# Normed tiles 1280 bytes apart, with weight blocks placed modulo 512 bytes

## The chip, the cores and the metric

One core of one Trainium2 chip runs the whole kernel. The metric is the device time in microseconds (us). It is given as a median of several runs. Differences are a few parts in a thousand, so the number of runs and their spread stand beside each time.

## The reference, cut to what matters

The program is two transformer blocks on one sequence of 256 positions, with 1024 channels, all in float32. The first block has an mLSTM and latent-attention mixer, a cross attention to 256 memory rows and a feed-forward of width 4096. The second block puts 16 meta tokens ahead of the sequence, so that it works on 272 positions, until these are dropped:

```
h = concatenate([meta, x])                                   # 16 + 256 positions
h = h + 0.5 * swiglu(rmsnorm(h, ffn1_norm), w_gate, w_up, w_down)      # width 2816
u = rmsnorm(h, mix_norm)
aq, ak, av, gq, gk, gv, gr, g_low, gate_a, gate_b = split(u @ w_in)    # 4368 columns
mixed = sigmoid(gate_a) * (window_attention(...) @ w_branch_att)
      + sigmoid(gate_b) * (gated_linear_attention(...) @ w_branch_gla)
h = h + mixed @ w_out
h = h + 0.5 * swiglu(rmsnorm(h, ffn2_norm), ...)
return rmsnorm(h, final_norm)[:, 16:]
```

Nearly all the work is the matrix products with weights. Their biggest one on 272 positions is the first SwiGLU of the second block: 1024 x 5632 weights for gate and up, then 2816 x 1024 for down.

## The kernel before, in words

Activations are kept transposed: 128 channels on the partitions, positions along them. An array of 1024 channels is eight tiles `k`. A product streams the tile of activations through TensorE against a stationary block of 128 x 128 weights. For float32 accuracy each value is split into a high part (float32r, rounded) and a low part, and three matmuls add up to one product: high weights on high activations (L1055), high weights on low activations (L1056), low weights on high activations (L1057). So each product of a weight block and a tile is three matmuls in a row, of 256 or 272 streamed columns.

`U` and `UL` hold the high and low parts of the normed input (eight tiles), `H` and `HLO` those of a hidden layer (22 tiles), `Y` and `YL` those of the mixers' outputs. Where a stage works on 256 positions, tile `k` of `U` begins 1024 `k` bytes after the first (`part`, L901). Where it works on 272 (`sw1`, `in2`, `gvr`, `gab`, read by `streamed`, L907), tile `k` begins 1088 `k` bytes after it. The products that need no meta columns (`NO_META`: gq, aq, gr, ga, gb) begin 64 bytes further in and stream 256 columns.

Weights come from HBM in units of at most 1024 columns (512 KB). `Gemm.units` (L173) says which rows of tiles `k` a unit holds: with 512 columns in a group, two. SyncE issues the loads in the order of `plan.loads` into six slots `raw` (`unit`, L2444); a load waits until the split of the unit six before it is done. ScalarE writes the high parts into `wh` (L1393), VectorE the low parts into `wl` (L1819); there are four halves for units that are split and not yet used up. TensorE then goes through the tiles of a unit: four blocks of 128 columns, for each its two `k`, for each three matmuls, 24 in all (`tile`, L1029). All groups of a product run after one another.

Where the blocks of a unit lie in `wh` and `wl` is decided by `first_columns` (L256), in steps of 16 columns, 64 bytes. For the products on 272 positions it shifts the block for tile `k` until its place is the place of tile `k` in `U` modulo 256 bytes. `same_place` (L196) orders the tiles so that a unit holds `k` and `k` + 4, which lie at the same place modulo 256 bytes. The first group of `sw1`, `in2` and `gvr` (`plain=1`) keeps the order 0, 1, 2, ..., because its tiles are only just being made. For `small`, `uv`, `o`, the feed-forward of the first block, `out2`, `sw2`, `dn2` and all others, `U`, `H` and the blocks lie at one place modulo 512 bytes without a shift, and `Y` at one of two places 256 bytes apart.

The order of the work is fixed by `Plan`: `first_block` and `second_mixer` weave the products with attention, mLSTM and gated linear attention by strings of letters (L117, L125), one letter for one step; the feed-forwards run straight through, except that one matmul against a block of ones in `cst` (`rstd_sum`, L1071, L1085) stands after 12 weight tiles of `ff1a` and after 9 of `sw1` and `sw2`. The mean square of the normed input comes from it. The gate matmul of the linear attention (`gla_logits`, L1240, L1244) waits for its weights `glagw`, which SyncE loads once (L2481).

The memory of a partition is laid out in `build` by the order of the calls of `sb`; each tensor begins at a multiple of 32 bytes. `beyond` puts a filler ahead of a tensor to bring the next address to a residue; `cst` is first, 5656 bytes long from byte 1152, then `vec` and seven small tensors, then X, U, UL, Y and the rest.

Of the kernel before, what the change touches and what calls it, by code (L numbers as in the profile page):

```python
# [14 lines left out]
P = 128  # L15
D = 1024
EPS = 1e-6
T1 = 256
T2 = 272
NMETA = 16  # L20
FF1 = 4096
# [158 lines left out]
def columns(w, n, width=512, r0=0):  # L180
    per = width // P
    return [([(w, r0, width * g, width)], [(128 * j, 128, per * g + j) for j in range(per)])
            for g in range(n // width)]
# [11 lines left out]

def same_place(n):  # L196

    pairs = [(8 * i + j, 8 * i + j + 4) for i in range((n + 7) // 8) for j in range(4) if 8 * i + j + 4 < n]
    order = [k for pair in pairs for k in pair]
    return order + [k for k in range(n) if k not in order]  # L200
# [21 lines left out]
    "ff2b": Gemm(2048, columns("w_ff2", D, r0=2048)),  # L222
    "sw1": Gemm(D, swiglu_columns("ffn1_w_gate_2", "ffn1_w_up_2"), same_place(8), plain=1),
    "dn1": Gemm(FF2, columns("ffn1_w_down_2", D), same_place(22)),
    "in2": Gemm(D, [([("w_in_2", 0, 2304, 16), ("w_in_2", 0, 2304, 16), ("w_in_2", 0, 768, 256)],
# [3 lines left out]
                    ([("w_in_2", 0, 0, 512)], [(128 * j, 128, ("aq", j)) for j in range(4)])], same_place(8), plain=1),  # L229
    "gvr": Gemm(D, wide("w_in_2", (("gv", 0, 1280), ("gr", 0, 1792))), same_place(8), plain=1),  # L230
    "gab": Gemm(D, wide("w_in_2", (("ga", 0, 2320), ("ga", 4, 2832), ("gb", 0, 3344), ("gb", 4, 3856))), same_place(8)),
    "branch": Gemm(512, [([(n, 0, 512 * g, 512)], [(128 * j, 128, (kind, 4 * g + j)) for j in range(4)])
# [23 lines left out]
def first_columns(name, g, i):  # L256


    ks, width = GEMM[name].units(g)[i], GEMM[name].width(g)
    skew = {"sw1": 0, "dn1": 0, "in2": g == 2, "gvr": g, "gab": 1}.get(name)  # L260
    at, shift = [], 0
    for n, k in enumerate(ks):
        while skew is not None and (n * width // 16 + shift - k - skew) % 4:
            shift += 1
        at.append(n * width + 16 * shift)
    return at
# [634 lines left out]
def part(t, name, k, n):  # L901

    at = SL * (k // 4) + n * (k % 4) if name in ("Y", "YL") else n * k
    return t[name].rearrange("p k c -> p (k c)")[:, at:at + n]


def streamed(t, name, k, tag):  # L907

    if name in ("small", "uv", "o", "wq_x", "ff1a", "ff1b", "sw2"):
        return part(t, "U", k, T1), part(t, "UL", k, T1)  # L910
    if name in ("sw1", "in2", "gvr", "gab"):
        a = NMETA if name != "sw1" and tag[0] in NO_META else 0
        return t["U"][:, k, a:T2], t["UL"][:, k, a:T2]
    if name in ("memk", "memv", "ff2a", "ff2b", "out2", "dn2"):
        return part(t, "H", k, T1), part(t, "HLO", k, T1)
    if name == "dn1":
        return t["H"][:, k, :], t["HLO"][:, k, :]
    if name in ("uq", "ukv"):
        k = 2 if name == "ukv" else k
        return t["CQH"][:, k, :], t["CQL"][:, k, :]  # L920
    return part(t, "Y", k, T1), part(t, "YL", k, T1)
# [1518 lines left out]
def sp_program(e, t, plan, ev):  # L2440
# [31 lines left out]
    for v in range(6, len(plan.loads)):  # L2472
        unit(v)
        if plan.loads[v] == ("ff1b", 0, 0):
            e.wait_ge(*at("mlstm_log", (3, 1)))
            e.wait_ge(*at("scores_masked", 3))
            e.wait_ge(*at("mlstm_sums", 3))
            e.dma_start(cst[:, OVER:OVER + NLATE], t["d_cst"][:, NCST:NCST + NLATE]).then_inc(
                *up("in_late", 0, by=16))
            e.wait_ge(*at("mlstm_qk", 3))  # L2480
            e.dma_start(t["glagw"][:, :], t["d_glagw"]).then_inc(*up("in_gg", 0, by=16))  # L2481
# [14 lines left out]
def build(nc, aps, out):  # L2496
    with ExitStack() as ctx:
# [9 lines left out]
        t["cst"] = sb("cst", [P, NCST])  # L2507
        t["vec"] = sb("vec", [P, NVEC])
        t["gcol"] = sb("gcol", [P, 8])
        t["DC"] = sb("DC", [P, 8])  # L2510
        t["ST"] = sb("ST", [P, 2, 6])
        t["ST2"] = sb("ST2", [P, 2, 16])
        t["nsink"] = sb("nsink", [P, 8])
        t["QRS"] = sb("QRS", [P, 8])
        t["QKG"] = sb("QKG", [P, 8])
        beyond(64, 256, "before_x")
        t["X"] = sb("X", [P, 8, T2])
        base = nc.sbuf_base
        for n in ("U", "UL"):
            t[n] = sb(n, [P, 8, T2], F32R)  # L2520

# [12 lines left out]
        t["G"] = sb("G", [P, 2, T2])  # L2534
        t["RM"] = sb("RM", [P, T2])
        beyond((base + 512) % 1024, 1024, "before_h")
# [18 lines left out]
        over(top_hlo, ("GT", [P, 6, 256], F32), ("PR", [P, 2, 512], F32), ("PT", [P, 2, 512], F32))  # L2555
        over(top_hlo, ("GQ1", [P, 2 * T1], F32))
        t["glagw"] = nc.alloc_sbuf_tensor_at("glagw", [P, 256], F32, offset=nc.sbuf_base)
        t["wqk"] = sb("wqk", [P, 4, 128])
        at = nc.sbuf_base
# [96 lines left out]
```

## Time and profile before

| | |
|---|---|
| runs | 922.36, 922.81, 924.12 us (median 922.81 of 3) |
| the profiled execution's own time | 922.65 us |
| its span, first to last instruction | 920.8 us |
| mean granted TensorE clock | 0.998 |
| matmul / weight load busy | 903.7 us (98%) / 886.0 us (96%), 7443 of each |
| VectorE / ScalarE busy | 642.5 us (70%) / 527.8 us (57%) |
| HBM read | 155.11 MB, 170 GB/s over the span |

The span leaves out what lies before the first and after the last instruction, here 1.85 us. A matmul of the trace is shown longer than the distance to the next one, since matmuls overlap in the array; so the pace is read from the starts, and the shown duration only tells one kind of matmul from another.

### The profile page before, as it was taken

The page shows a single profiled execution, that of the slowest core. Times are in us where ns is not written, and L with a number is a line of the kernel's source. Part 1 is how long each engine was busy: PE and PEld are TensorE (multiplying, and loading weights), DVE is VectorE, ACT ScalarE, POOL GpSimd, SP SyncE. Part 2 cuts the span into 40 slices and gives each one's busy share as a digit, 9 for nine tenths or more (in the row PEclk, how much of TensorE's full clock was granted, in tenths as well). Part 3 has the DMA queues.
Part 4 walks back from the last instruction along what each step waited for, and adds up shares of the span by engine and source line. Part 5 has one row for each costly group of instructions (what it writes and reads, how often), then busy time and mean ns, then how long its engine had stood idle before and what let it go on. Part 6 is the DMA issues. An engine that isn't in the chain of part 4 may idle for free.

```text
span 920.8 us, 18474 instructions
## 1 busy us (share of the span) xinstructions
PE 903.7 (98%) x7443; PEld 886.0 (96%) x7443; DVE 642.5 (70%) x1092; ACT 527.8 (57%) x862; POOL 3.5 (0%) x9
## 2 busy tenths in 40 slices
PE   8999999999999999999999999999999999999996
PEld 7987999899999999999999999999999999999996
DVE  5999778777556766666666548768769867767553
ACT  5788867776436655544444435454675665454452
POOL 1000000000000000000000000000000000000000
PEclk9999999999999999999999999999999999999999
DMA  9651435265665566555556565554416665666641
GB/s 330 222 177 38 130 114 192 53 227 198 206 209 168 190 201 192 174 172 175 181 184 198 153 183 163 158 174 126 159 47 192 198 183 184 191 200 201 210 138 47
DMA packets 110292, 157.37 MB, mean 171 GB/s; under 512 B 9728, under 2 KB 61056, under 8 KB 110080
## 3 DMA queue, kind: packets, MB, share of 16 engines
q1 hardware_dynamic: 109632, 155.22, 53.5%
q8 instruction: 60, 0.98, 0.4%
q10 hardware_dynamic: 576, 0.96, 0.3%
q14 instruction: 24, 0.20, 0.1%
HBM read 155.11 MB, written 1.05 MB: 170 GB/s over the span
## 4 chain that ended last, share of the span: by engine, by line
PE 95%; DVE 2%; ACT 1%; issue 1%; DMA 1%; SPq 0%; DVEq 0%; ACTq 0%
PE ps L1055 29%; PE ps L1057 29%; PE ps L1056 29%; PE ps L1102 1%; PE ps L1138 1%; DMA X<-d_x 1%; PE ps L1314 0%; PE ps L1334 0%; DVE wl L1819 0%; PE ps L1272 0%; PE ps L1335 0%; ACT wh L1393 0%; PE ps L1294 0%; PE ps L1148 0%; PE ps L1161 0%
## 5 line engine op out<-in xcount | busy, mean ns | idle before, releaser
L1819 DVE TENSOR_TENSOR wl<-raw,wh 128x1024 fp32r<-128x1024 f32 (+2 forms) x291 | 346.1, 1212 | 192.3 <-ACT wh L1393 192.0
L1393 ACT ACTIVATE wh<-raw 128x1024 fp32r<-128x1024 f32 (+2 forms) x291 | 297.9, 1046 | 190.7 <-PE ps L1057 190.3
L1055 PE MATMUL ps<-U,wh 128*128 128x256 f32 (+2 forms) x1392 | 396.5, 285 | 4.9 <-DVE wl L1819 3.3
L1057 PE MATMUL ps<-U,wl 128*128 128x256 f32 (+2 forms) x1392 | 390.3, 280 | 0.0
L1056 PE MATMUL ps<-UL,wh 128*128 128x256 f32 (+2 forms) x1392 | 389.6, 280 | 0.0
L1055 PEld LDWEIGHTS ps<-U,wh 128*128 128x128 f32 (+1 forms) x1392 | 261.7, 188 | 8.0 <-DVE wl L1819 6.3
L1056 PEld LDWEIGHTS ps<-UL,wh 128*128 128x128 f32 (+1 forms) x1392 | 261.7, 188 | 1.1 <-issue 0.5
L1057 PEld LDWEIGHTS ps<-U,wl 128*128 128x128 f32 (+1 forms) x1392 | 261.2, 188 | 0.0
L1055 PE MATMUL ps<-H,wh 128*128 128x256 f32 (+1 forms) x736 | 207.6, 282 | 0.0
L1057 PE MATMUL ps<-H,wl 128*128 128x256 f32 (+1 forms) x736 | 205.3, 279 | 0.0
L1056 PE MATMUL ps<-HLO,wh 128*128 128x256 f32 (+1 forms) x736 | 205.0, 279 | 0.0
L1056 PEld LDWEIGHTS ps<-HLO,wh 128*128 128x128 f32 x736 | 138.4, 188 | 0.8 <-issue 0.7
L1055 PEld LDWEIGHTS ps<-H,wh 128*128 128x128 f32 x736 | 138.3, 188 | 0.8 <-issue 0.7
L1057 PEld LDWEIGHTS ps<-H,wl 128*128 128x128 f32 x736 | 138.3, 188 | 0.0
L1055 PE MATMUL ps<-Y,wh 128*128 128x256 f32 x160 | 46.6, 291 | 0.0
L1507 ACT ACTIVATE H<-S 128x272 fp32r<-128x272 f32 (+1 forms) x44 | 18.7, 425 | 45.7 <-DVE S L2006 45.7
L1056 PE MATMUL ps<-YL,wh 128*128 128x256 f32 x160 | 44.4, 278 | 0.0
L1057 PE MATMUL ps<-Y,wl 128*128 128x256 f32 x160 | 44.4, 278 | 0.0
L2055 DVE TENSOR_TENSOR HLO<-S,H 128x256 fp32r<-128x256 f32 (+1 forms) x84 | 35.8, 426 | 7.6 <-ACT H L1495 4.2
L1503 ACT ACTIVATE S<-S 128x272 f32<-128x272 f32 (+1 forms) x44 | 18.7, 425 | 33.4 <-DVE S L2001 33.4
L1479 ACT ACTIVATE U<-X,vec 128x256 fp32r<-128x256 f32 (+1 forms) x40 | 20.5, 512 | 21.2 <-DVE X L1979 12.9
L1055 PEld LDWEIGHTS ps<-Y,wh 128*128 128x128 f32 x160 | 30.1, 188 | 1.1 <-issue 1.0
(337 smaller groups left out, 800.3 us busy)
## 6 DMA issues: line engine op xcount, KB each, us to landing
raw<-w_ff SPq DMA_DIRECT2D x64, 512.0 KB, 4.3
raw<-ffn_w_gate SPq DMA_DIRECT2D x88, 256.0 KB, 3.6
raw<-ffn_w_up SPq DMA_DIRECT2D x88, 256.0 KB, 4.6
raw<-ffn_w_down SPq DMA_DIRECT2D x44, 512.0 KB, 4.5
raw<-w_in SPq DMA_DIRECT2D x40, 512.0 KB, 4.0
raw<-w_out SPq DMA_DIRECT2D x16, 512.0 KB, 4.2
raw<-wkv_x SPq DMA_DIRECT2D x8, 512.0 KB, 4.1
raw<-w_in SPq DMA_DIRECT2D x9, 256.0 KB, 3.1
```

The source lines that it names most:

```text
L1055: e.matmul(out, sh, xh, start=(i == 0 and n == 0), stop=False)
L1056: e.matmul(out, sh, xl, start=False, stop=False)
L1057: mm = e.matmul(out, sl, xh, start=False, stop=(over and n == nk - 1))
L1102: e.matmul(pb, cst("halves" if tag in ("kr", "qr") else "ones"), sq[:, a:z], start=True, stop=True).then_inc(*up("norm_sum", (tag, i)))
L1138: mm = e.matmul(ps[:, o:o + n], q(h, a0, a0 + 128), k(h, 0, n), start=(i == 0), stop=(i == len(pairs) - 1))
L1393: e.activation(wh, raw, ACT.Copy).then_inc(*up("w_hi", v))
L1479: e.activation(part(t, "U", k, n), xs, ACT.Identity, scale=vec(GAIN[stage], k)).then_inc(*up("u_hi", (stage, k)))
L1503: e.activation(S(i, T2, T2 + T), S(i, 0, T), ACT.Silu).then_inc(*up("silu", (name, n)))
L1507: e.activation(part(t, "H", n, T), S(i, 2 * T2, 2 * T2 + T), ACT.Copy).then_inc(*up("h_hi", (name, n)))
L1819: lo = e.tensor_tensor(wl, raw, wh.bitcast(F32), ALU.subtract)
L2055: e.tensor_tensor(part(t, "HLO", n, T), full, part(t, "H", n, T).bitcast(F32), ALU.subtract).then_inc(*up("h_lo", (name, n)))
```

## The change

It has four parts.

1. In the products on 272 positions `U` and `UL` keep tile `k` 1280 bytes (`WIDE` = 320 columns) apart instead of 1088. Both tensors grow from 8704 to 10752 bytes (`NU` = 2688 columns).
2. Units of `sw1`, `in2`, `gvr` and `gab` hold `k` and `k` + 2 (which lie 2560 bytes apart) instead of `k` and `k` + 4, beyond the plain groups. `dn1`, which streams `H`, keeps its order and its 1088 bytes.
3. Their weight blocks are shifted until they lie at the tile's place modulo 512 bytes instead of 256.
4. To make room, `wqk`, `vec`, `RM` and seven small tensors move into the ends of `U` and `UL`, and `glagw` into a region above `HLO`'s tiles in use. Its load, which stood after the first load of `ff1b`, now stands after that of `("in2", 1, 0)` and waits for the end of `dn1`.

```diff
-def same_place(n):
-    pairs = [(8 * i + j, 8 * i + j + 4) for i in range((n + 7) // 8) for j in range(4) if 8 * i + j + 4 < n]
+def same_place(n, apart):
+    pairs = [(k, k + apart) for k in range(n - apart) if k // apart % 2 == 0]
...
-    "sw1": Gemm(D, swiglu_columns("ffn1_w_gate_2", "ffn1_w_up_2"), same_place(8), plain=1),
-    "dn1": Gemm(FF2, columns("ffn1_w_down_2", D), same_place(22)),
+    "sw1": Gemm(D, swiglu_columns("ffn1_w_gate_2", "ffn1_w_up_2"), same_place(8, 2), plain=1),
+    "dn1": Gemm(FF2, columns("ffn1_w_down_2", D), same_place(22, 4)),
...
-        while skew is not None and (n * width // 16 + shift - k - skew) % 4:
+        place, modulus = (17 * k, 4) if name == "dn1" else (WIDE // 16 * k, 8)
+        while skew is not None and (n * width // 16 + shift - place - skew) % modulus:
             shift += 1
...
+    if name in ("U", "UL"):
+        at = (WIDE if n == T2 else n) * k
+        return t[name][:, at:at + n]
...
-        return t["U"][:, k, a:T2], t["UL"][:, k, a:T2]
+        return part(t, "U", k, T2)[:, a:T2], part(t, "UL", k, T2)[:, a:T2]
...
-            e.wait_ge(*at("mlstm_qk", 3))
+        if plan.loads[v] == ("in2", 1, 0):
+            e.wait_ge(*at("gemm", ("end", "dn1")))
             e.dma_start(t["glagw"][:, :], t["d_glagw"]).then_inc(*up("in_gg", 0, by=16))
...
-        t["vec"] = sb("vec", [P, NVEC])
-        t["gcol"] = sb("gcol", [P, 8])
...
         beyond(64, 256, "before_x")
         t["X"] = sb("X", [P, 8, T2])
         base = nc.sbuf_base
-        for n in ("U", "UL"):
-            t[n] = sb(n, [P, 8, T2], F32R)
+        for n, named in (("U", (("wqk", [P, 4, 128]), ("vec", [P, NVEC]))),
+                         ("UL", (("RM", [P, T2]), ("gcol", [P, 8]), ("DC", [P, 8]), ("ST", [P, 2, 6]),
+                                 ("ST2", [P, 2, 16]), ("nsink", [P, 8]), ("QRS", [P, 8]), ("QKG", [P, 8])))):
+            at = nc.sbuf_base
+            t[n] = sb(n, [P, NU], F32R)
+            for i, (small, shape) in enumerate(named):
+                off = 8 * T1 * 4 if i == 0 else max(off, (7 * WIDE + T2) * 4)
+                t[small] = nc.alloc_sbuf_tensor_at(small, shape, F32, offset=at + off)
+                off += (int(np.prod(shape[1:])) * 4 + 31) // 32 * 32
...
-        over(top_hlo, ("GQ1", [P, 2 * T1], F32))
-        t["glagw"] = nc.alloc_sbuf_tensor_at("glagw", [P, 256], F32, offset=nc.sbuf_base)
-        t["wqk"] = sb("wqk", [P, 4, 128])
+        over(top_hlo, ("GQ1", [P, 2 * T1], F32), ("glagw", [P, 256], F32))
```

## Rows read from the trace of the kernel before

**Rows 1.** The page, part 1: busy time, share and instructions of each engine.
```profile
PE 903.7 (98%) x7443; PEld 886.0 (96%) x7443; DVE 642.5 (70%) x1092; ACT 527.8 (57%) x862; POOL 3.5 (0%) x9
```

**Rows 2.** The page, part 4: the chain that ended last.
```profile
PE 95%; DVE 2%; ACT 1%; issue 1%; DMA 1%; SPq 0%; DVEq 0%; ACTq 0%
```

**Rows 3.** Waits of TensorE over the span, the longest: total us, times, longest.
```profile
PE ps L1055 <- DVE wl L1819: 3.3, 4, 1.4
```

**Rows 4.** Timeline of TensorE (start us, shown us): first matmuls of stages.
```profile
271.08 0.28 PE L1055 MATMUL ps<-U,wh 128*128 128x256 f32 x1
...
358.12 0.28 PE L1055 MATMUL ps<-U,wh 128*128 128x272 f32 x1
...
364.15 0.28 PE L1055 MATMUL ps<-U,wh 128*128 128x272 f32 x1
...
370.63 0.28 PE L1055 MATMUL ps<-U,wh 128*128 128x272 f32 x1
...
489.36 0.29 PE L1055 MATMUL ps<-H,wh 128*128 128x272 f32 x1
...
519.04 0.29 PE L1055 MATMUL ps<-H,wh 128*128 128x272 f32 x1
...
522.04 0.29 PE L1055 MATMUL ps<-H,wh 128*128 128x272 f32 x1
```

**Rows 5.** Line L1055, 227.9 to 357 us: durations ns min/median/max, starts.
```profile
L1055 PE MATMUL ps<-H,wh x252: 276/276/276, 227.9 to 356.8; 128*128 128x256 f32 x126
L1055 PEld LDWEIGHTS ps<-H,wh x252: 187/188/188, 228.1 to 357.0; 128*128 128x128 f32 x126
```

**Rows 6.** Line L1055 in `wq_x`, 153.02 to 155.85 us.
```profile
L1055 PEld LDWEIGHTS ps<-U,wh x8: 192/192/192, 152.9 to 155.4; 128*128 128x128 f32 x8
L1055 PE MATMUL ps<-U,wh x8: 281/281/281, 153.0 to 155.5; 128*128 128x256 f32 x8
```

**Rows 7.** Timeline of TensorE: start and end of that stretch of `wq_x`.
```profile
153.02 0.28 PE L1055 MATMUL ps<-U,wh 128*128 128x256 f32 x1
...
155.85 0.38 PE L1085 MATMUL ps<-ACC,cst 128*128 128x256 f32 x1
```

**Rows 8.** Line L1055 in `branch`, 692 to 709 us.
```profile
L1055 PE MATMUL ps<-Y,wh x51: 276/276/276, 691.8 to 708.8; 128*128 128x256 f32 x51
```

**Rows 9.** Line L1056 in the second mixer, 589.3 to 593.3 and 593.4 to 598.9 us.
```profile
L1056 PE MATMUL ps<-UL,wh x12: 276/276/279, 589.4 to 593.1; 128*128 128x256 f32 x12
...
L1056 PE MATMUL ps<-UL,wh x17: 276/281/283, 593.1 to 598.8; 128*128 128x256 f32 x17
```

**Rows 10.** Groups by line and shape (busy us, mean ns), 573.5 to 686 us.
```profile
L1056 PE MATMUL ps<-UL,wh 128*128 128x256 f32 x189 | 52.9, 280 | 0.0
```

**Rows 11.** The same view, 20 to 160 us.
```profile
L1056 PE MATMUL ps<-UL,wh 128*128 128x256 f32 x129 | 35.9, 278 | 0.0
...
L1056 PE MATMUL ps<-YL,wh 128*128 128x256 f32 x64 | 17.9, 280 | 0.0
```

**Rows 12.** Timeline of SyncE's queue and VectorE around the end of `dn1`.
```profile
551.77 0.47 SPq L2457 DMA_DIRECT2D raw<-w_in  x1
...
552.93 1.06 DVE L1819 TENSOR_TENSOR wl<-raw,wh 128x864 fp32r<-128x864 f32 x1 [1.61 <-ACT wh L1393]
...
554.26 0.37 SPq L2457 DMA_DIRECT2D raw<-w_in  x1
```

**Rows 13.** Timeline of TensorE: end of `dn1`, and the gate matmul.
```profile
554.72 0.29 PE L1055 MATMUL ps<-U,wh 128*128 128x272 f32 x1
...
572.60 1.08 PE L1244 MATMUL ps<-G,glagw 128*128 128x272 f32 x4
```

**Rows 14.** Tile `glagw`: its load, and the time to landing.
```profile
L2481 SPq DMA_DIRECT2D glagw<-d_glagw x1: 431/431/431, 250.1 to 250.1; - x1
...
DMA to landing us min/median/max: 4.8/4.8/4.8
```

**Rows 15.** Timeline of TensorE: the ones-block matmul inside `ff1a`.
```profile
191.76 0.59 PE L1085 MATMUL ps<-ACC,cst 128*128 128x256 f32 x2
```

More of the change, by code:

```diff
@@ L19 @@
 T2 = 272
+WIDE = 320
+NU = 2688
 NMETA = 16
@@ L228 @@
                      [(0, 128, ("gk", 0)), (128, 128, ("gk", 1)), (256, 128, ("ak", 0)), (384, 128, ("av", 0))]),
-                    ([("w_in_2", 0, 0, 512)], [(128 * j, 128, ("aq", j)) for j in range(4)])], same_place(8), plain=1),
-    "gvr": Gemm(D, wide("w_in_2", (("gv", 0, 1280), ("gr", 0, 1792))), same_place(8), plain=1),
-    "gab": Gemm(D, wide("w_in_2", (("ga", 0, 2320), ("ga", 4, 2832), ("gb", 0, 3344), ("gb", 4, 3856))), same_place(8)),
+                    ([("w_in_2", 0, 0, 512)], [(128 * j, 128, ("aq", j)) for j in range(4)])], same_place(8, 2), plain=1),
+    "gvr": Gemm(D, wide("w_in_2", (("gv", 0, 1280), ("gr", 0, 1792))), same_place(8, 2), plain=1),
+    "gab": Gemm(D, wide("w_in_2", (("ga", 0, 2320), ("ga", 4, 2832), ("gb", 0, 3344), ("gb", 4, 3856))), same_place(8, 2)),
     "branch": Gemm(512, [([(n, 0, 512 * g, 512)], [(128 * j, 128, (kind, 4 * g + j)) for j in range(4)])
@@ L2507, in build @@
         t["cst"] = sb("cst", [P, NCST])
-        t["vec"] = sb("vec", [P, NVEC])
-        t["gcol"] = sb("gcol", [P, 8])
[L2510 to L2515, printed above, removed]
         beyond(64, 256, "before_x")
@@ L2518, in build @@
         base = nc.sbuf_base
-        for n in ("U", "UL"):
-            t[n] = sb(n, [P, 8, T2], F32R)
+        for n, named in (("U", (("wqk", [P, 4, 128]), ("vec", [P, NVEC]))),
[7 more added lines that the diff above has]
+                off += (int(np.prod(shape[1:])) * 4 + 31) // 32 * 32
+            assert off <= NU * 4
         for i, n in enumerate(("Y", "YL")):
@@ L2534, in build @@
         t["G"] = sb("G", [P, 2, T2])
-        t["RM"] = sb("RM", [P, T2])
         beyond((base + 512) % 1024, 1024, "before_h")
```

## Prediction

> **What bounds the kernel.** I read the busy times first: TensorE is busy 98% of the span, VectorE 70% [rows 1]. The chain that ended last lies on TensorE for 95% [rows 2], and its longest wait by cause is 3.3 us in all, in the first microseconds [rows 3]. So the time is the number of matmuls times the distance from one start to the next. Nothing is added or taken away by this change, so only the distance can move the time; it is read from starts.
>
> From 271.08 to 358.12 us run `ff1b` and `ff2b`, 768 matmuls of 256 columns: 87.04 / 768 = 113.33 ns each [rows 4]. The clock is 2.4 GHz there (0.998 granted over the span), so that is 272 cycles, 16 more than columns. If 272 columns also cost 16 more, they would take 288 cycles or 120.0 ns. They take more. Groups 1 to 10 of `sw1`: 489.36 - 370.63 = 118.73 us for 960, 123.68 ns. The first two units of `sw1`'s group 0: 6.03 us for 48, 125.6 ns. Ten units of `dn1`: 29.68 us for 240, 123.67 ns; its last unit of the group, which holds k 18 and 19: 3.00 us for 24, 125.0 ns [rows 4]. Clock and engine are the same in all of these; what differs is how often the streamed place steps by 64 bytes: once in three matmuls in group 0 and in unit (18, 19), once in 24 elsewhere.
>
> Matmuls of 256 columns show a second thing: two paces at one arrangement. The fast one shows 276 ns for the matmul and 188 for its weight load [rows 5]. In `wq_x` the durations are 281 and 192 [rows 6], and 24 matmuls take 2.83 us, 117.9 ns each [rows 7], though nothing there lies otherwise than in `ff1b`. A pace, once on, stays till something interrupts it.
>
> **The change, part by part.** (a) *Steps of 64 bytes vanish.* After the change all places of a stage are equal modulo 256 bytes. A line through 125.6 ns at 1/3 step per matmul and 123.68 at 1/24 has slope 6.6 ns per step; with `dn1`'s 125.0 it is 4.6. Without steps that leaves 123.4 to 123.5; I take 123.45. Gain: 960 x 0.23 = 0.22 us in `sw1`, 96 x 2.15 = 0.21 in its group 0, the same 0.2 in `gvr`'s group 0, which has the same order, and 96 x 0.23 = 0.02 in `in2`'s group 1. Sum 0.65 us. `dn1` keeps its layout: nothing.
>
> (b) *Equal modulo 512 in place of 256.* This is the disputed term. Bounds: below, it takes 272 columns down to the 120.0 ns of the 16-cycle rule; above, the pace of steadily misplaced tiles, 125.6. Before, the tile k + 4 lies 256 bytes off its place modulo 512 against the block, the tile k does not; if that hurt, it would hurt 256 columns too. `branch` alternates between just these two relations of `Y` and block, and shows 276 ns throughout [rows 8]. I take zero.
>
> (c) *256-column products of the second mixer*: 624 matmuls (gab 384, gvr's second group 96, in2 144). They sit mostly in the slow pace: mean duration 280 against 276 and 281, so 0.8 of them [rows 10]. In the first block, woven as much but without 64-byte steps, U's show 278, Y's 280 [rows 11], 0.4 to 0.8. One place in the mixer shows why: 276 up to 593.1 us in the unit of aq with tiles 0 and 4, and 281 right after it, when the unit of tiles 1 and 5 begins, 64 bytes on [rows 9]. With steps of 256 bytes only, I take a slow share of 0.5: 0.3 x 624 x (117.9 - 113.3) = 0.86 us gained; ends 0 (share stays 0.8) and 2.3 (none slow), and a loss of 0.6 if all are slow. I take 0.85.
>
> (d) *The load of `glagw` and its wait.* Queued behind it on SyncE are all later weight loads. The load of ("in2", 1, 0) issues at 551.8; the next one waits for the split that ends at 552.93 + 1.06 and issues at 554.26 [rows 12]. `dn1` ends at about 555.0 [rows 13]. So SyncE stands from 552.2 to 555.0, issues `glagw` in 0.4, and the next load goes out some 1.2 us late, at 555.5. VectorE splits that unit only after 570, fifteen microseconds on, and the later loads wait for splits after 559 anyway. If that cover were gone it would cost these 1.2 us once. `glagw` took 4.8 us to land [rows 14]: 560, against a use at 572.60 [rows 13]. Cost nothing; the issue saved at 250 us was hidden too.
>
> (e) *Moved tensors.* The splits write the same number of columns with another stride, the norms' outputs too: VectorE at 70% and ScalarE at 57% cover them. `cst` ends at byte 6808, the filler begins at 6816 and is 168 bytes, so X begins at 7008 and U at 15712, which is 96 modulo 256, where before it was 64. Streams, blocks and hidden tiles move together; only `cst` stays. I take zero, and come back to it below.
>
> Sum: 0.65 + 0.85 = 1.5 us. Against the profiled execution's own 922.65 us (span 920.8, 1.85 around it), that is 921.15; that execution lies 0.16 under the median of the runs. About 0.2% (1.85 us) is what a measurement of this kernel can tell from no change, the spread of the runs shown being 1.76.
>
> **Rivals.** *Modulo 512 counts at 272 columns.* For: no 272-column stretch before is equal modulo 512 for more than three matmuls, so the trace cannot exclude it. Against: rows 8. Then 960 x 3.68 + 96 x 5.6 + 96 x 5.6 + 96 x 3.7 = 4.96 us, with (c) 5.8: 916.8.
>
> *Places don't matter.* Then all paces come from history alone: 922.65. Against it: the excess grows with the steps [rows 4]. The Trainium skill (SBUF — State Buffer, section "Who interferes with whom") gives TensorE two independent read ports, one for the streamed operand and one for weight loads, and says that it never waits on anyone; by that rule this change moves nothing, and the sum would be zero. Here the trace disagrees with the rule as far as it shows two paces for one shape [rows 5, 6].
>
> *A long stage resumes at the slow pace*, which ends slower. The place is the matmul against the ones-block at 191.76 us [rows 15]; 1464 matmuls of 256 columns follow it to 358 without another interruption, all at the fast pace now. `cst` does not move with the streams, so the pause can end in another phase. Price: 1464 x 4.6 = 6.7 us, 921.15 + 6.7 = 927.9. It decides from some 330 slow matmuls on (1.5 / 4.6 ns). The same can happen in `sw2`. For: in `wq_x` the slow pace held till L1085 came [rows 7]. Against: the relation modulo 64 bytes is all that is new there. A cousin is 32 bytes costing every stream a little, for which no row exists.
>
> **How the numbers follow.** Forecast (a with c) 0.58, at 921.2; modulo 512 counts 0.15; places don't matter 0.11; slow stage 0.16. The forecast's own range is 919 to 923, by the ends of (c) and the chance in paces. The whole range reaches to 916.5 for the first rival and to 924.5; the slow stage is left out. Against the median 922.81, faster by over 0.2% means under 920.96: 0.27 of the forecast's 0.58 and the first rival, 0.42. Slower, over 924.66: 0.16. Within: 0.42.
>
> **What would show it.** Right: `sw1` from its group 1 on takes 118.4 to 118.6 us in place of 118.73, its first 48 matmuls 5.93 in place of 6.03; `dn1` as before; 113.33 ns in `ff1a` to `ff2b` and `sw2`; mean 278 or 279 for 256 columns in the mixer; SyncE standing till `dn1`'s end, with TensorE never waiting there. Wrong: `sw1` near 115.2 us (first rival) or above 119; durations of 281 in `ff1` or `sw2`; a wait before L1244.

## The result, and the profile after

The changed kernel takes 935.34 us (median of 4 runs: 932.17, 932.65, 938.03, 938.03) against 923.15 for the kernel before (4 runs, 922.36 to 924.12). The ratio is 1.013, 95% interval 1.0086 to 1.0175: slower, where 921.2 was forecast and the range ended at 924.5. The four runs lie at two levels, at about 932.4 and at 938.0. The profiled execution is one of the lower level, 932.17 us with a span of 930.4, 9.6 more than before; it had the same granted clock, 0.998.

First the page of the changed kernel: part 1, then part 4. (A helper added ahead of them moves the code: L1063 to L1065 are L1055 to L1057 of before, L1093 is L1085, L1827 is L1819.)

```profile
PE 913.2 (98%) x7443; PEld 895.3 (96%) x7443; DVE 642.5 (69%) x1092; ACT 528.8 (57%) x862; POOL 3.5 (0%) x9
...
PE 95%; DVE 2%; ACT 1%; issue 1%; DMA 1%; SPq 0%; DVEq 0%; ACTq 0%
```

The number of matmuls is the same and the chain still lies on TensorE for 95%, as in [rows 1, 2]; TensorE is busy 9.5 us longer. So the pace changed. These are the starts that answer to [rows 4], then those of `branch`, `out2`, `sw2` and `dn2`, from the timeline of TensorE of the changed kernel (start us, shown us):

```profile
272.39 0.28 PE L1063 MATMUL ps<-U,wh 128*128 128x256 f32 x1
...
359.43 0.28 PE L1063 MATMUL ps<-U,wh 128*128 128x272 f32 x1
...
365.35 0.29 PE L1063 MATMUL ps<-U,wh 128*128 128x272 f32 x1
...
371.74 0.29 PE L1063 MATMUL ps<-U,wh 128*128 128x272 f32 x1
...
490.14 0.29 PE L1063 MATMUL ps<-H,wh 128*128 128x272 f32 x1
...
519.82 0.29 PE L1063 MATMUL ps<-H,wh 128*128 128x272 f32 x1
...
522.81 0.29 PE L1063 MATMUL ps<-H,wh 128*128 128x272 f32 x1
...
686.93 0.28 PE L1063 MATMUL ps<-Y,wh 128*128 128x256 f32 x1
...
711.73 0.28 PE L1063 MATMUL ps<-H,wh 128*128 128x256 f32 x1
...
734.34 0.28 PE L1063 MATMUL ps<-U,wh 128*128 128x256 f32 x1
...
859.14 0.28 PE L1063 MATMUL ps<-H,wh 128*128 128x256 f32 x1
```

The last four of them, in the kernel before:

```profile
686.25 0.28 PE L1055 MATMUL ps<-Y,wh 128*128 128x256 f32 x1
...
710.19 0.28 PE L1055 MATMUL ps<-H,wh 128*128 128x256 f32 x1
...
731.95 0.28 PE L1055 MATMUL ps<-U,wh 128*128 128x256 f32 x1
...
852.07 0.28 PE L1055 MATMUL ps<-H,wh 128*128 128x256 f32 x1
```

Set against the same starts of before, they show where the 9.6 us come in (`ff1a` and `gab` are read in the same way):

| stage begins | before | after | later by |
|---|---|---|---|
| `ff1a` | 183.60 | 184.58 | 0.98 |
| `ff1b` | 271.08 | 272.39 | 1.31 |
| `sw1` | 358.12 | 359.43 | 1.31 |
| `dn1` | 489.36 | 490.14 | 0.78 |
| first `gab` | 571.90 | 572.55 | 0.65 |
| `branch` | 686.25 | 686.93 | 0.68 |
| `out2` | 710.19 | 711.73 | 1.54 |
| `sw2` | 731.95 | 734.34 | 2.39 |
| `dn2` | 852.07 | 859.14 | 7.07 |
| end of the span | 920.8 | 930.4 | 9.6 |

`sw1` gave back 0.53 us, where 0.43 was forecast. The 0.98 us ahead of `ff1a` lie in stages woven with attention and mLSTM, and no run explains them: over all profiles `ff1a` begins between 183.38 and 185.01 us, and the changed kernel profiled again (e12) gives 185.01 where this one gives 184.58. But from `branch` to the end 8.9 us are lost. The shown durations say of what kind: line L1064 of the changed kernel from 194 to 227, 228 to 357, 695 to 711 and 743 to 880 us (durations ns min/median/max, first and last start):

```profile
L1064 PE MATMUL ps<-UL,wh x98: 276/276/276, 194.0 to 226.9; 128*128 128x256 f32 x98
...
L1064 PE MATMUL ps<-HLO,wh x249: 276/276/276, 229.0 to 356.8; 128*128 128x256 f32 x125
...
L1064 PE MATMUL ps<-YL,wh x46: 281/281/281, 694.9 to 710.8; 128*128 128x256 f32 x46
...
L1064 PE MATMUL ps<-UL,wh x329: 281/281/281, 743.0 to 858.9; 128*128 128x256 f32 x165
L1064 PE MATMUL ps<-HLO,wh x59: 281/281/281, 859.3 to 879.8; 128*128 128x256 f32 x59
```

This is the slow pace of [rows 6, 7], now through four whole stages. `branch` ran at 276 ns before [rows 8], and so did `sw2` and `dn2`; line L1056 of the kernel before, from 743 to 880 us:

```profile
L1056 PE MATMUL ps<-UL,wh x321: 276/276/276, 743.0 to 851.8; 128*128 128x256 f32 x161
```

The granted clock is 1.00 from 742 to 859 us in the changed kernel, so it isn't the clock. Groups 1 to 10 of `sw2` (746.08 to 859.14 us) give 113.06 / 960 = 117.77 ns from start to start, against 113.33. With 192 matmuls in `branch`, 192 in `out2`, 1056 in `sw2` and 528 in `dn2` that is 1968 x 4.45 = 8.8 us: the loss. The minimum is the median and the maximum, so it is no mixture. And it begins at one instruction. The timeline of TensorE of the changed kernel, last gate tile and first matmuls of `branch`:

```profile
686.48 0.28 PE L1065 MATMUL ps<-U,wl 128*128 128x256 f32 x1
686.59 0.28 PE L1063 MATMUL ps<-U,wh 128*128 128x256 f32 x1
686.71 0.28 PE L1064 MATMUL ps<-UL,wh 128*128 128x256 f32 x1
686.82 0.28 PE L1065 MATMUL ps<-U,wl 128*128 128x256 f32 x1
686.93 0.28 PE L1063 MATMUL ps<-Y,wh 128*128 128x256 f32 x1
687.05 0.28 PE L1064 MATMUL ps<-YL,wh 128*128 128x256 f32 x1
687.17 0.28 PE L1065 MATMUL ps<-Y,wl 128*128 128x256 f32 x1
687.29 0.28 PE L1063 MATMUL ps<-Y,wh 128*128 128x256 f32 x1
```

686.48 to 686.93 is 0.45 us for four matmuls; 686.93 to 687.29 is 0.36 for three, so 113 ns each and then some 119. Nothing stands between. What changes there is the place. A gate tile begins 1280 k + 64 bytes into `U`, so every one now lies 64 bytes beyond the place modulo 256 at which `Y`, `H` and their blocks lie. Before, the last unit was that of k 3 and 7, and 1088 x 7 + 64 = 7680 is a multiple of 256: no step into `branch`.

That names two suspects: this step, and the 32 bytes by which the large tensors moved against `cst`. The second can act at the ones-block matmul, which stands in `ff1a`, `sw1` and `sw2`; the program issues it once, and the trace shows it as two records [rows 15].

### The profile page after: what moved, and what is told of

It is laid out like the page before. It is cut to its first block, busy times and chain, and to the rows that moved or that the text cites. A ratio compares the mean times of both kernels' runs of the same rounds, so it can differ in the third digit from the quotient of the medians.

```text
span 930.4 us, 18474 instructions
## 1 busy us (share of the span) xinstructions
PE 913.2 (98%) x7443; PEld 895.3 (96%) x7443; DVE 642.5 (69%) x1092; ACT 528.8 (57%) x862; POOL 3.5 (0%) x9
## 4 chain that ended last, share of the span: by engine, by line
PE 95%; DVE 2%; ACT 1%; issue 1%; DMA 1%; SPq 0%; DVEq 0%; ACTq 0%
PE ps L1063 29%; PE ps L1065 29%; PE ps L1064 29%; PE ps L1110 1%; PE ps L1146 1%; DMA X<-d_x 1%; PE ps L1322 0%; PE ps L1342 0%; DVE wl L1827 0%; PE ps L1280 0%; PE ps L1343 0%; ACT wh L1401 0%; PE ps L1302 0%; PE ps L1156 0%; PE ps L1169 0%
## 5 line engine op out<-in xcount | busy, mean ns | idle before, releaser
L1827 DVE TENSOR_TENSOR wl<-raw,wh 128x1024 fp32r<-128x1024 f32 (+2 forms) x291 | 346.2, 1212 | 200.2 <-ACT wh L1401 200.0
L1063 PE MATMUL ps<-U,wh 128*128 128x256 f32 (+2 forms) x1392 | 398.4, 286 | 4.9 <-DVE wl L1827 4.9
L1065 PE MATMUL ps<-U,wl 128*128 128x256 f32 (+2 forms) x1392 | 391.8, 281 | 0.0
L1064 PE MATMUL ps<-UL,wh 128*128 128x256 f32 (+2 forms) x1392 | 391.8, 281 | 0.0
L1063 PEld LDWEIGHTS ps<-U,wh 128*128 128x128 f32 (+1 forms) x1392 | 261.6, 188 | 8.1 <-DVE wl L1827 6.5
L1065 PEld LDWEIGHTS ps<-U,wl 128*128 128x128 f32 (+1 forms) x1392 | 263.2, 189 | 0.0
L1064 PEld LDWEIGHTS ps<-UL,wh 128*128 128x128 f32 (+1 forms) x1392 | 261.5, 188 | 1.1 <-issue 0.5
L1063 PE MATMUL ps<-H,wh 128*128 128x256 f32 (+1 forms) x736 | 208.8, 284 | 0.0
L1065 PE MATMUL ps<-H,wl 128*128 128x256 f32 (+1 forms) x736 | 206.5, 281 | 0.0
L1064 PE MATMUL ps<-HLO,wh 128*128 128x256 f32 (+1 forms) x736 | 206.3, 280 | 0.0
L1065 PEld LDWEIGHTS ps<-H,wl 128*128 128x128 f32 x736 | 139.3, 189 | 0.0
L1064 PEld LDWEIGHTS ps<-HLO,wh 128*128 128x128 f32 x736 | 138.5, 188 | 0.8 <-issue 0.7
L1063 PEld LDWEIGHTS ps<-H,wh 128*128 128x128 f32 x736 | 138.3, 188 | 0.8 <-issue 0.7
L1063 PE MATMUL ps<-Y,wh 128*128 128x256 f32 x160 | 47.1, 295 | 0.0
L1065 PE MATMUL ps<-Y,wl 128*128 128x256 f32 x160 | 45.0, 281 | 0.0
L1064 PE MATMUL ps<-YL,wh 128*128 128x256 f32 x160 | 44.9, 281 | 0.0
L1063 PEld LDWEIGHTS ps<-Y,wh 128*128 128x128 f32 x160 | 30.1, 188 | 1.1 <-issue 1.0
```

The lines of the kernel that those rows point to most:

```text
L1063: e.matmul(out, sh, xh, start=(i == 0 and n == 0), stop=False)
L1064: e.matmul(out, sh, xl, start=False, stop=False)
L1065: mm = e.matmul(out, sl, xh, start=False, stop=(over and n == nk - 1))
L1827: lo = e.tensor_tensor(wl, raw, wh.bitcast(F32), ALU.subtract)
```

## The experiments

All kernels compute the whole reference. In each the time is the median of its runs, and the ratio is taken against the kernel before on the same chip at the same time: 923.42 us beside e1 to e4, 923.03 beside e5 to e8, 923.24 beside e9 to e11. "Slow" means 281 ns shown and 117.78 ns from start to start, "fast" 276 and 113.33.

**e1, the step removed.** In the changed kernel the tiles go 192 bytes further in, so that 192 + 64 is 256 and the gate tiles lie at `Y`'s place; blocks follow modulo 256.

```diff
-    skew = {"sw1": 0, "dn1": 0, "in2": g == 2, "gvr": g, "gab": 1}.get(name)
+    skew = {"sw1": 3, "dn1": 0, "in2": 4 if g == 2 else 3, "gvr": 4 if g else 3, "gab": 4}.get(name)
...
-        place, modulus = (17 * k, 4) if name == "dn1" else (WIDE // 16 * k, 8)
+        place, modulus = (17 * k, 4) if name == "dn1" else (WIDE // 16 * k, 4)
...
-        at = (WIDE if n == T2 else n) * k
+        at = 48 + WIDE * k if n == T2 else n * k
...
```

> The changed kernel, with the tiles on 272 positions begun 192 bytes further in, so that the part without meta columns lies where the tiles of 256 positions lie modulo 256 bytes; the blocks follow (placed modulo 256 bytes). Entering branch from the last gate products is then no step of 64 bytes. Theory A (that step turns the fast pace into the slow one, and it stays to the end): branch, out2, sw2 and dn2 run at 113.3 ns a matmul again (276 ns shown) and the time falls by 8.7 us in the profiled execution, to about 921 to 924 us, leaving a second level some 6 us higher if ff1a to ff2b can still fall into the slow pace by themselves. Theory B (the 32 bytes by which everything but the constants moved set the slow pace): no change, 932 to 938 us, since those 32 bytes stay. Theory C (pure chance of the interruptions): either, with several levels among the runs.

Measured: 929.1 us (928.9 to 929.51 in five runs, and 934.74), ratio 1.0071, interval 1.0054 to 1.0088. Its profiled execution is the one of 934.74. Line L1064 there, in `ff1a` ahead of the ones-block matmul at 192.04 us, behind it, in `ff2a` and `ff2b`, in `branch`, and in `sw2` ahead of the ones-block matmul at 743.27:

```profile
L1064 PE MATMUL ps<-UL,wh x21: 276/276/277, 184.0 to 190.8; 128*128 128x256 f32 x21
...
L1064 PE MATMUL ps<-UL,wh x94: 281/281/282, 194.0 to 226.9; 128*128 128x256 f32 x94
...
L1064 PE MATMUL ps<-HLO,wh x234: 281/281/282, 229.3 to 356.9; 128*128 128x256 f32 x117
...
L1064 PE MATMUL ps<-YL,wh x42: 276/276/280, 691.5 to 707.7; 128*128 128x256 f32 x42
...
L1064 PE MATMUL ps<-UL,wh x9: 276/276/277, 737.3 to 740.0; 128*128 128x256 f32 x9
```

`branch` and `out2` are back at 113.3 ns, so the step was what slowed them. But `ff1a` goes from 276 to 281 ns at the ones-block matmul and stays there to 357 us (117.79 ns from start to start), and `sw2` and `dn2` turn slow at theirs. The start of `sw1` is at 364.90 us, 5.47 later than in the profile of the changed kernel, which is about the distance between its two levels, 5.6.

**e2, the 32 bytes taken back.** The changed kernel with a filler that puts X at 64 modulo 256 again.

```diff
-        beyond(64, 256, "before_x")
+        sb("before_x", [P, 40])
```

> The changed kernel with a filler of 160 bytes ahead of X, so that X, U and all behind them begin at 64 modulo 256 bytes again, as before, in place of 96. All steps stay as in the changed kernel. Theory A: branch to dn2 stay slow, 932 us at the lower level. Theory B: fast again, 921 to 923 us. For the upper level (938 us in two of four runs of the changed kernel, where I suppose ff1a to ff2b slow, 1464 matmuls by 4.4 ns = 6.5 us): it goes away if the 32 bytes against the constants make it, and stays if not.

Measured: 924.25 us (923.8 to 925.3, 11 runs), ratio 1.0009 (1.0001 to 1.0018), so all but 1 us of the loss is gone, and the second level with it. Line L1064, in `branch`, in `sw2` ahead of the ones-block matmul at 739.23 us and behind it:

```profile
L1064 PE MATMUL ps<-YL,wh x49: 281/281/282, 690.9 to 707.9; 128*128 128x256 f32 x49
...
L1064 PE MATMUL ps<-UL,wh x19: 278/281/282, 733.0 to 739.8; 128*128 128x256 f32 x19
L1064 PE MATMUL ps<-UL,wh x328: 275/276/277, 741.8 to 853.0; 128*128 128x256 f32 x164
```

The step still slows `branch` and `out2`. What is new is that the ones-block matmul in `sw2` now ends it. The same instruction turns slow into fast here, and fast into slow in e1.

**e3, only the memory moved.** The changed kernel with tiles 1088 bytes apart, units of k and k + 4 and blocks modulo 256, as before; the moved tensors and fillers stay.

```diff
-WIDE = 320
+WIDE = 272
...
-    "sw1": Gemm(D, swiglu_columns("ffn1_w_gate_2", "ffn1_w_up_2"), same_place(8, 2), plain=1),
+    "sw1": Gemm(D, swiglu_columns("ffn1_w_gate_2", "ffn1_w_up_2"), same_place(8, 4), plain=1),
...
-        place, modulus = (17 * k, 4) if name == "dn1" else (WIDE // 16 * k, 8)
+        place, modulus = (17 * k, 4) if name == "dn1" else (WIDE // 16 * k, 4)
```

> Only the memory plan of the changed kernel (larger U and UL, small tensors in their ends, the late load of the gate weights, everything 32 bytes on), with the tiles 1088 bytes apart, units of k and k + 4 and blocks modulo 256 bytes as before. The last gate tile, k = 7, then lies where Y lies modulo 256 bytes. Theory A: fast from branch on, near 922.5 us at the lower level, sw1 back at 130.9 us. Theory B: slow, 931 us or more.

Measured: 936.62 us (930.4, 936.32, 936.92, 937.13), ratio 1.0127 (1.0104 to 1.015). The move alone costs most of what the whole change costs, again at two levels 6 us apart, each 1 to 2 us under that of the changed kernel: it lacks the step into `branch`, and the gain in `sw1` too. In its profile `branch` and `out2` are at 276 ns, `ff1a` behind the ones-block to `ff2b`, and `sw2` behind it and `dn2`, at 281.

**e4, the step put into the kernel before.** Only the order of `gab`'s tiles: it ends with k 6, whose gate tile lies 192 bytes off modulo 256, so that `branch` begins 64 bytes on.

```diff
-    "gab": Gemm(D, wide("w_in_2", (("ga", 0, 2320), ("ga", 4, 2832), ("gb", 0, 3344), ("gb", 4, 3856))), same_place(8)),
+    "gab": Gemm(D, wide("w_in_2", (("ga", 0, 2320), ("ga", 4, 2832), ("gb", 0, 3344), ("gb", 4, 3856))), [3, 7, 0, 4, 1, 5, 2, 6]),
```

> The kernel before, with the units of the gate products in the order (3,7), (0,4), (1,5), (2,6) in place of (0,4), (1,5), (2,6), (3,7). Nothing else moves, but branch is now entered from tile 6, 64 bytes off its own place, where it was entered from tile 7, in place. Theory A: if the last gate products run at the fast pace, branch to dn2 turn slow: 923 + 8.7 = about 931.7 us. If they run slow, either may follow. Theories B and C: 922 to 924 us as before.

Measured: 924.95 us (924.34 to 925.76, 10 runs), ratio 1.0018 (1.0008 to 1.0027), 1.5 us over the median of before. `branch` and `out2` take 117.8 ns and `sw2` is fast behind its ones-block matmul. In its profile the two stages take 47.40 us in place of 45.70. So the step costs 384 x 4.45 = 1.7 us there and 0.2 in the first 54 matmuls of `sw2`, and no more, as long as `cst` lies as before.

**e5, `cst` moved along.** The changed kernel with 32 bytes ahead of `cst`, which puts the ones-block back at the place of the weight blocks modulo 256.

```diff
+        sb("before_cst", [P, 8])
```

> The changed kernel with 32 bytes ahead of cst, so that the constants move by the same 32 bytes as X and all behind it: the block of ones lies where the weight blocks lie modulo 256 bytes again, as before, while everything is 32 bytes off a multiple of 64. Theory B1 (what counts is where the ones-block lies against the streams and blocks around it: its matmul L1085 resets the pace, to fast if in place): ff1a from L1085 on, ff2a, ff1b, ff2b and sw2 from its L1085 on, dn2 at 113.3 ns, only branch and out2 slow by the step; about 924.3 us, without levels. Theory B2 (addresses 32 off a multiple of 64 are bad by themselves): slow from L1085 on, 930 to 938 us.

Measured: 923.98 us (923.57 to 925.48, 10 runs), ratio 1.0012 (1.0003 to 1.0021). X is still at 96 modulo 256 here. It is not the place of the streams that hurts, but their distance from `cst`. Only `branch`, `out2` and the first tiles of `sw2` stay slow.

**e6, both mended.** The edits of e1 and the filler of e2 together.

> The changed kernel with both mends: X and all behind it at 64 modulo 256 bytes, and the tiles on 272 positions 192 bytes further in, so that branch is entered in place. Both theories: branch, out2, sw2, dn2 and ff1a to ff2b fast. Against e2 (924.25 us) 383 matmuls of branch and out2 by 4.45 ns = 1.7 us less: 922.5 us, 0.1% under the kernel before, whose gain is the 0.7 us of sw1 and gvr.

Measured: 921.19 us (920.58 to 921.55, 11 runs), ratio 0.998 (0.9971 to 0.9989). This is faster than the kernel before, by 0.2%, and it is the time that was forecast for the change. The page of this kernel, then line L1064 from 228 to 357, in `branch` and from 742 to 880 us:

```profile
PE 902.7 (98%) x7443; PEld 884.6 (96%) x7443; DVE 642.4 (70%) x1092; ACT 527.9 (57%) x862; POOL 3.5 (0%) x9
...
L1064 PE MATMUL ps<-HLO,wh x252: 276/276/276, 228.0 to 356.9; 128*128 128x256 f32 x126
...
L1064 PE MATMUL ps<-YL,wh x50: 276/276/276, 691.0 to 707.7; 128*128 128x256 f32 x50
...
L1064 PE MATMUL ps<-UL,wh x320: 276/276/276, 741.8 to 850.2; 128*128 128x256 f32 x160
```

All long stages are at 113.33 ns. The mean from start to start in `sw1` is 123.34 ns, though its blocks are only equal modulo 256.

**e7, `cst` moved the other way.** The kernel before with 32 bytes ahead of `cst`: the ones-block lies 32 bytes beyond the weight blocks' place, where in the changed kernel it lies 32 short of it.

```diff
+        sb("before_cst", [P, 8])
```

> The kernel before with 32 bytes ahead of cst and nothing else: X and all behind it stay at 64 modulo 256 bytes, the block of ones lies 32 bytes off. Theory B1: L1085 leaves ff1a to ff2b or sw2 to dn2 or both slow in most executions, 929 to 936 us. Theory B2: as before, 923 us.

Measured: 923.15 us (922.41 to 923.6, 10 runs), ratio 1.0001 (0.9992 to 1.001). No cost. So not every distance hurts. (Here and in e10 and e11 `vec` and the seven small tensors move with `cst`.)

**e8, all but `cst` moved, in the kernel before.** The filler ahead of X, 96 bytes in this kernel, becomes one of 128. That moves X and all behind it by 32 bytes, as in the changed kernel.

```diff
-        beyond(64, 256, "before_x")
+        sb("before_x", [P, 32])
```

> The kernel before with 32 more bytes of filler ahead of X and nothing else: X, U, blocks, H at 96 modulo 256 bytes (blocks at 160), the constants where they were. Theory B in both forms: 929 to 937 us, as the kernel with only its memory moved. If it stays at 923 us, something else of the moved memory is the cause (the late gate load, the small tensors at the ends of U and UL).

Measured: 930.59 us (930.32 to 930.89, 4 runs), ratio 1.0084 (1.007 to 1.0097). Line L1056 of this kernel, ahead of and behind the ones-block matmul at 193.04 us, then the same for the one at 739.36:

```profile
L1056 PE MATMUL ps<-UL,wh x18: 281/281/281, 184.7 to 190.7; 128*128 128x256 f32 x18
...
L1056 PE MATMUL ps<-UL,wh x98: 276/276/276, 193.9 to 226.9; 128*128 128x256 f32 x98
...
L1056 PE MATMUL ps<-UL,wh x19: 276/276/281, 733.4 to 739.9; 128*128 128x256 f32 x19
...
L1056 PE MATMUL ps<-UL,wh x328: 281/281/281, 742.0 to 857.6; 128*128 128x256 f32 x164
```

Here one execution shows both turns: the matmul turns slow into fast at 193 us and fast into slow at 739.

**e10 and e11, the constants at other distances.** The kernel before with 224 bytes ahead of `cst` (the ones-block at -32 modulo 256), and with 128 (half way round). In both, X and all behind it move by 256 bytes, so they stay where they were modulo 256.

```diff
+        sb("before_cst", [P, 56])
```

```diff
+        sb("before_cst", [P, 32])
```

> The kernel before with 224 bytes ahead of cst: the block of ones lies at 96 modulo 256 bytes against weight blocks at 128, the same relation modulo 256 as in the slow kernels (128 against 160), while X and all behind it stay at 64. If the relation modulo 256 decides: L1085 in sw2 leaves the slow pace (sw2, dn2 117.8 ns), and in ff1a it turns slow into fast and fast into slow, so 929 to 937 us in levels 6 us apart. If the multiple of 64 of the streams counts as well: 923 us.

> The kernel before with 128 bytes ahead of cst: the block of ones at 0 modulo 256 bytes against blocks at 128. No row tells this relation. If only the 32 bytes short of place are bad: 923 us. If being out of place in general is bad except 32 bytes beyond it: 929 us or more.

Measured: at -32, 936.45 us (930.68, 936.25, 936.65, 936.99), ratio 1.0129 (1.0104 to 1.0154), at two levels 6 us apart again. At -128, 925.7 us (924.94 to 925.92, 9 runs), ratio 1.0025 (1.0015 to 1.0035): both long runs behind the ones-block matmul fast, but `branch` and `out2` at 117.8 ns. They arrive slow there from the mixer, with no step of 64 bytes at their entry, and only the ones-block matmul in `sw2` ends it.

**e9, the identity in place.** In the mended kernel e6 the products woven into the mixers still take 115 to 117 ns. The suspicion was the identity and the other blocks of `cst` that the mixer's own steps use. A gap in `cst` puts them at the weight blocks' place. The diff is against e6.

```diff
-for _n, _w in (("ones", 128), ("invf", 1), ("shift", 1), ("turn", 1), ("sign", 1), ("eps", 1), ("one", 1), ("ident", 128), ("halves", 128),
+for _n, _w in (("ones", 128), ("invf", 1), ("shift", 1), ("turn", 1), ("sign", 1), ("eps", 1), ("one", 1), ("gap", 58), ("ident", 128), ("halves", 128),
...
-        sb("before_x", [P, 40])
+        sb("before_x", [P, 48])
```

> The kernel with both mends (e6, 921.19 us), and 58 unused columns in cst after its single columns, so that the identity, the halves and the other blocks of constants also begin where the weight blocks do modulo 256 bytes; the identity lay 24 bytes past such a place. They are streamed or loaded in the transposes and sums that interrupt the products of both mixers. If the place of the interrupting block sets the pace that follows there too, uv, memk, memv, w_out, wq_x, gab, gvr and in2 move from 115 to 118 ns towards 113.5: at most 1100 matmuls by some 3 ns, 3 us; 918 to 920 us. If the pace there is set by when the interruption comes: 921.2 us, unchanged.

Measured: 921.85 us (920.89 to 923.68, 11 runs), ratio 0.9987 (0.9979 to 0.9996). `gab` is at 115.5 ns where it was at 115.4, `w_out` at 116.6 against 117.1 (means over the intervals in which nothing else runs). It gained nothing; the pace in the woven stages isn't set by the place of these blocks alone.

**e12, the changed kernel once more**, for a second profile.

> The changed kernel as it is, for a second profile. By the theory that the ones-block matmul in ff1a flips the pace when the block lies 32 bytes before the weight blocks modulo 256: every execution is at one of two levels. At the lower one (932 to 933 us) ff1a after the ones-block to ff2b show 276 ns and 113.33 ns from start to start; at the upper one (938) they show 281 ns and 117.78, and the stages up to the ones-block arrive fast. branch, out2, sw2 and dn2 are at 117.78 in both. The rival, that the upper level has another cause, expects a profile at 938 with ff1 at 113.33.

Measured: 932.63 and 938.26 us, against 922.88 before (3 runs); ratio 1.0136 (1.0064 to 1.0208). The profiled execution was again one of the lower level, and shows the same mean pace as the first in every stage from `ff1a` on. The two levels are confirmed, but the upper one of this very kernel was not seen from inside, so the test that this run was made for stays undone.

## Why the prediction was wrong

Taken together the runs show what the ones-block matmul does. Its block lies at a distance modulo 256 from the place of the weight blocks:

| distance | kernels | behind it in `ff1a` | behind it in `sw2` |
|---|---|---|---|
| 0 | before, e2, e4, e5, e6, e9 | fast | fast |
| +32 | e7 | fast | fast |
| -128 | e11 | fast | fast |
| -32 | after, e12, e1, e3, e8, e10 | slow if it arrived fast (e1, e3), fast if slow (after, e12, e8, e10) | slow, from either |

The two columns of the last row need not mean that the stages differ. The weight loads show that the slow pace comes in more than one kind: of the three matmuls of a product, the load of one shows 192 ns and those of the other two 188, and in a fast stretch all three show 188 (medians). Ahead of the ones-block matmul in `ff1a` every slow profile has the 192 on the second matmul; in `branch`, `out2`, `sw2` and `dn2`, and in `ff1a` to `ff2b` of e1 and e3, it is on the third. In the changed kernel, L1064 from 185 to 192 us, then L1065 ahead of and behind the ones-block matmul in `sw2`:

```profile
L1064 PEld LDWEIGHTS ps<-UL,wh x20: 192/192/192, 184.9 to 191.7; 128*128 128x128 f32 x20
...
L1065 PEld LDWEIGHTS ps<-U,wl x15: 192/192/192, 734.8 to 739.8; 128*128 128x128 f32 x15
...
L1065 PEld LDWEIGHTS ps<-U,wl x329: 192/192/192, 743.0 to 858.9; 128*128 128x128 f32 x165
```

So at -32 the ones-block matmul turned fast into slow in both stages (two profiles of two in `ff1a`, four of four in `sw2`), the slow pace with 192 on the second into fast (four of four), and left the one with 192 on the third slow (after and e12). No run brought the second kind into `sw2` or the third into `ff1a`, so whether the kind or the stage decides is not shown.

**Step (e), moved tensors, "I take zero", is what failed.** The text had the 32 bytes and had `cst` staying behind, and still priced them at nothing. They cost (1002 + 528) x 4.45 = 6.8 us in `sw2` and `dn2`, in each of the six profiles at -32 (e8, whose only change they are, is 7.6 us over the median of before; 6.9 of the 8.2 us by which its span is longer lie in `sw2` and behind it). In the executions of the upper level they cost nearly as much again in `ff1a` to `ff2b`. That the upper level of the changed kernel is this is inferred. e1 and e3 were profiled at their own upper levels and show it, and up to `sw1` they issue what the changed kernel issues, with only a few small tensors at other places. The distance fits: 5.47 us to the start of `sw1` against 938.03 - 932.17 = 5.86. By this reading the level is picked by whether `ff1a` is entered fast or slow, and that varies without any change: the kernel before and e4, the same up to `gab`, enter it fast (276 ns) and slow (281 ns).

**The rival "a long stage resumes at the slow pace"** had the cause: the ones-block matmul, `cst` not moving with the streams. It was given 0.16 and left out of the range. Its price, 1464 x 4.6 = 6.7 us, was also good; 1464 x 4.45 = 6.5 less what a fast arrival saves. But it placed this in `ff1a` alone and called `sw2` "the same can happen", unpriced. `sw2` with `dn2` is the place where it happens always. Its argument against, that the relation modulo 64 bytes is all that is new, was no argument: no run of the kernel before had tried another relation.

**The step into `branch` was missed.** Part (a) says that after the change "all places of a stage are equal modulo 256 bytes". That is right within a stage and says nothing of the seam between two. The gate tiles all moved 64 bytes off the place of everything else, and the last of them meets `branch`. Priced by e4: 1.7 us. In the changed kernel the step also means that `sw2` arrives slow, but with the block at -32 it would leave slow in any case (e1, e8).

**(a) Steps vanish: right.** `sw1` from its group 1 on takes 490.14 - 371.74 = 118.40 us (forecast 118.4 to 118.6), 123.33 ns; its first 48 matmuls 365.35 - 359.43 = 5.92 (5.93). The means of all intervals give 0.53 us in `sw1`, 0.16 in `gvr` and 0.04 in `in2`, together 0.73 against 0.65; the pace without steps is 123.33 ns, a little under the 123.45 taken. The last unit of `dn1`'s group, whose layout stayed, takes 2.99 against 3.00.

**(b) Modulo 512: right at zero.** Over all its intervals `sw1` takes 123.34 ns with blocks equal modulo 512, and 123.34 in e6 with blocks equal modulo 256. The 120.0 ns of the sixteen-cycle rule came nowhere.

**(c) The second mixer: not gained.** Over the intervals in which nothing else runs `gab` takes 116.9 ns against 117.0, `in2`'s 256 columns 118.0 against 116.9. From 574 to 687 us the changed kernel shows, in the view by line and shape, what [rows 10] show:

```profile
L1064 PE MATMUL ps<-UL,wh 128*128 128x256 f32 x190 | 53.2, 280 | 0.0
```

The step was moved from between the tiles to between these products and all others. With their tiles in place the mean falls to 115.4 in `gab` and 115.1 in `in2` (e6; e2, which differs from e6 by this and by the blocks' modulus, stays at 117.1 and 118.0); 384 x 1.6 + 144 x 1.8 is 0.87 us. So places do act in the woven stages, and by about what the term was priced at, but only once these tiles also lie where the others do, which the prediction did not ask for; that the sizes agree is in part luck. With 0.73 from (a) it makes 1.6 us of the 1.8 by which e6 is faster than the kernel before.

**(d) `glagw`: right.** The timeline of SyncE's queue at the end of `dn1`, and the landing of tile `glagw`, in the changed kernel:

```profile
552.12 0.88 SPq L2465 DMA_DIRECT2D raw<-w_in  x2
555.68 0.34 SPq L2490 DMA_DIRECT2D glagw<-d_glagw  x1
556.06 6.22 SPq L2465 DMA_DIRECT2D raw<-w_in  x3
...
DMA to landing us min/median/max: 2.1/2.1/2.1
```

The queue stands from 553.0 to 555.7, the next weight load goes out at 556.06 (forecast 555.5), and `glagw` has landed at 557.8, fifteen microseconds ahead of its use at 573.2. TensorE waits for none of it.

The rival that places don't matter is refuted: a kernel that differs from the one before by 56 columns of filler is 1.3% slower (e10). It rested on the Trainium skill (SBUF — State Buffer, "Who interferes with whom"), by which TensorE reads streamed operand and weights through independent ports and never waits on another. The trace doesn't contradict it about other engines; but two paces for one shape, 113.33 and 117.78 ns, which a filler decides, are something that the rule has no room for.

What stays open: why a block 32 bytes short of the others acts as it does and one 32 beyond or 128 off does not, and what the distances never tried would do; whether the distance that counts is that to the weight blocks, to the streamed tiles or to `ACC`, which moved together in every run; whether the kind of slow pace or the stage decides what the ones-block matmul leaves; what sets the pace inside the woven stages, where the same kernel comes out differently from step to step, and with it whether `ff1a` is entered fast or slow; and why `branch` is entered slow in e11, where there is no step.

## What to carry to other kernels

A change of layout is priced at its seams too: list the place of each operand modulo 256 at every passage from one product to the next and around every single matmul that interrupts a stream, and treat a row that has never been tried as a risk and not as zero. When tensors are moved, hold the relation of the constants to the streams; fillers must be counted with the allocator's rounding (here the formula counted from byte 6808 and meant X to begin at 6976, 64 modulo 256; it began at 7008). And where a stage is long, a pace lost at its first instruction costs its whole length: here a single matmul decided over some 1,500 others, twice.

## What the runs showed of the hardware

Matmuls of 128 x 128 float32r weights with 256 columns run at one of two paces from start to start, 113.33 or 117.78 ns, at the same clock and, within a stage, the same addresses. The trace shows the pace in each matmul's record (276 or 281 ns), and in one weight load of three: in every slow stretch of `ff1a` to `ff2b` and of `branch` to `dn2` the load of one and the same of the three matmuls has a median of 192 ns and those of the others 188, and in every fast stretch all three have 188. In [rows 6] it is the load of the first. A pace holds over more than a thousand matmuls (1530 in `sw2` and `dn2` of e8), through stages with other operands, until something interrupts it. With 272 columns and no steps only one steady pace was seen, 123.33 ns, whether the stage ahead ran at the slow pace (e1) or the fast one. A step of 64 bytes at full stream turned fast into slow in four kernels of four (after, e2, e4, e5). A single matmul with another block can turn it either way, and the kernels that differ in little but the place of that block modulo 256 (before, e7, e10, e11) show that this place has a part in it.
